# Moving the opening of a second transformer block into the last layer of the first

## The reference

```
x = layer_norm(DN_ALPHA * x + mix, ln1_g[l], ln1_b[l])
x = layer_norm(DN_ALPHA * x + swiglu(x, ffn_w1[l], ffn_w3[l], ffn_w2[l]), ln2_g[l], ln2_b[l])
```

```
mod   = silu(c)     @ w_ada + b_ada          # six parts of 1024: shift, scale, gate, twice
mod_c = silu(c_ctx) @ w_ada + b_ada
h_ctx = norm(ctx) * (1 + sc1c) + sh1c        # norm: plain layer norm, no gain, no bias
h_x   = norm(x)   * (1 + sc1)  + sh1
proj  = concat(h_ctx, h_x) @ w_in            # 512 tokens, 3936 columns
```

## Time and profile before

| what | value |
|---|---|
| time, median of 3 runs | 2152.38 us (2146.57, 2152.41, 2152.38) |
| time of the profiled execution | 2147.28 us |
| its span (first to last instruction) | 2145.2 us, so 2.08 us lie around it |
| PE, DVE, ACT, POOL busy | 95%, 40%, 22%, 12% of the span |
| mean granted TensorE clock | 0.979 of full speed |

### The profile page before, as it was taken

One profiled execution on the slowest core, in us unless ns is written; L12 is line 12 of the kernel. 1 busy time (PEld: TensorE's weight loads), 2 busy tenths in 40 slices (PEclk: granted clock), 3 DMA queues, 4 the chain that ended last, 5 costly groups with the idle time before them and its releaser, 6 DMA issues.

```text
span 2145.2 us, 33503 instructions
## 1 busy us (share of the span) xinstructions
PE 2046.7 (95%) x13831; PEld 1383.0 (64%) x13831; DVE 852.9 (40%) x1551; ACT 469.5 (22%) x881; POOL 250.7 (12%) x233
## 2 busy tenths in 40 slices
PE   8999999999999999999899999999997999999996
PEld 5678868864768868884445555899975444344342
DVE  1794220002379131000458847545557223323324
ACT  2254100000426201000132134432332110110110
POOL 2783000000478100000000002000000000000000
PEclk9999999999999999999899999999996999999998
DMA  7332544344533344435712333300013899999993
GB/s 240 118 118 99 201 152 151 124 168 133 175 118 118 116 179 157 157 118 180 262 70 79 118 118 124 114 4 4 3 44 136 353 410 395 393 395 411 394 392 143
DMA packets 138697, 385.37 MB, mean 180 GB/s; under 512 B 16935, under 2 KB 64399, under 8 KB 127441
## 3 DMA queue, kind: packets, MB, share of 16 engines
q1 hardware_dynamic: 138577, 383.61, 48.1%
HBM read 382.54 MB, written 1.05 MB: 179 GB/s over the span
## 4 chain that ended last, share of the span: by engine, by line
PE 42%; DVE 5%; ACT 2%; issue 1%; DMA 0%; DVEq 0%; POOL 0%; ACTq 0%; POOLq 0%
PE psum L1297 9%; PE psum L2874 9%; PE psum L2044 8%; PE psum L2898 5%; PE psum L2809 3%; PE psum L1496 1%; PE psum L2460 1%; ACT arena L1654 1%; PE psum L2113 1%; DVE arena L3087 1%; DVE arena L3009 1%; PE psum L2886 1%; PE psum L2062 1%; PE psum L2827 0%; DMA ring<-in_w_ada_dram 0%
## 5 line engine op out<-in xcount | busy, mean ns | idle before, releaser
L383 PE MATMUL psum<-arena,ring 128*128 128x256 f32 x1728 | 382.3, 380 | 1.0 <-ACT arena L666 1.0
L383 PEld LDWEIGHTS psum<-arena,ring 128*128 128x128 f32 x1728 | 324.5, 189 | 55.4 <-issue 8.6
L602 PE MATMUL psum<-arena,ring 128*128 128x256 f32 (+1 forms) x1536 | 306.8, 361 | 3.6 <-ACT arena L657 3.6
L602 PEld LDWEIGHTS psum<-arena,ring 128*128 128x128 f32 x1536 | 270.8, 190 | 39.3 <-issue 2.3
L2044 PE MATMUL psum<-arena 64*64 64x64 f32 (+1 forms) x4320 | 180.0, 237 | 4.2 <-DVE arena L2269 1.5
L2044 PEld LDWEIGHTS psum<-arena 64*64 64x64 f32 x4320 | 171.7, 134 | 6.3 <-issue 2.7
L666 ACT ACTIVATE arena<-psum 128x512 f32<-128x512 f32 (+2 forms) x100 | 54.4, 563 | 507.3 <-PE psum L602 264.1
L629 PE MATMUL psum<-ring,arena 128*128 128x512 f32 x352 | 151.7, 593 | 0.0
L1297 PE MATMUL psum<-arena,ring 128*128 128x512 f32 (+2 forms) x432 | 142.2, 489 | 0.0
L1067 DVE TENSOR_TENSOR arena<-arena,psum 128x512 f32<-128x512 f32 x22 | 15.2, 690 | 289.2 <-PE psum L602 289.2
L1297 PEld LDWEIGHTS psum<-arena,ring 128*128 128x128 f32 (+1 forms) x432 | 80.7, 187 | 61.3 <-issue 55.7
(11 more groups left out here) (418 smaller groups left out, 2585.5 us busy)
## 6 DMA issues: line engine op xcount, KB each, us to landing
ring<-in_w_in_dram SPq DMA_DIRECT2D x29, 2048.0 KB, 8.3
ring<-in_ffn_w_dram SPq DMA_DIRECT2D x46, 1024.0 KB, 5.5
arena<-in_ex_gate_dram SPq DMA_DIRECT2D x15, 2048.0 KB, 11.6
arena<-in_ex_up_dram SPq DMA_DIRECT2D x15, 2048.0 KB, 16.1
arena<-in_ex_down_dram SPq DMA_DIRECT2D x15, 2048.0 KB, 18.0
ring<-in_ex_gate_dram SPq DMA_DIRECT2D x14, 2048.0 KB, 10.9
ring<-in_ex_up_dram SPq DMA_DIRECT2D x14, 2048.0 KB, 15.4
ring<-in_ex_down_dram SPq DMA_DIRECT2D x14, 2048.0 KB, 8.1
```

The source lines that it names most:

```text
L383: ins = pe.matmul(bank[:, j, :], w[:, kc, c * P:(c + 1) * P], moving[:, kc, :], start=kc == 0, stop=kc == k - 1)
L602: ins = pe.matmul(bank[:, j, tokens], both[:, i * DC + kc, j * P:(j + 1) * P], K.xT[:, kc, tokens], start=kc == 0, stop=kc == DC - 1)
```

## The change

It moves parts of the second block's opening into the last layer and its feed-forward part:
- PE does the three transposes of the small rows after unit 3 of `ffn_w2`, into the two `next` banks; the eight `next` transposes no longer run in the last layer.
- ACT makes the conditioning vector right after the last `f1` drain (`mid_open_scalar`), and takes the root for the context norm.
- DVE does the whole context norm (`second_norm(0)`) before the last layer's second norm, and the second block's norm of token tile 0 (`second_norm(1)`) between that layer's norms of tile 0 and tile 1. Only tile 1 (`second_norm(2)`) is left for after it.
- ada units 0 and 1 are loaded into tiles that are dead by then (`K.early`), with no wait for a ring slot; the ring begins with ada 2, ada 3 and `w2in` 7, which are issued before the wait for the finished `x_in`.
- The transposes of `x` go by token tile; the gate columns are copied between the context's and `x`'s drains; POOL clears all but one tile earlier. Some tiles lie elsewhere, and the mid groups get other banks.

```diff
--- before.py
+++ after.py
@@ -635,14 +635,24 @@
         for u in range(W2_UNITS - 2):
             pe.wait_ge(K.landed(("w2", u)), K.landed_count(("w2", u), l))
             down(u, list(banks)).then_inc(K.used_up(("w2", u)), 1)
+        if l == DEPTH - 1:
+            pe.wait_ge(K.sem["dma_vec"], K.count("dma_vec"))
+            for i in range(2):
+                pe.wait_ge(K.empty(("next", i)), K.empty_count(("next", i), l))
+            pe.transpose(K.bank(("next", 0))[:, 0:P], K.vrows2, ident).then_inc(K.full(("next", 0)), 1)
+            bank = K.bank(("next", 1))
+            pe.transpose(bank[:, 0:P], K.crows[:, 0, :], ident)
+            n = 9 * CONV_CHUNKS - P
+            pe.transpose(bank[:, P:P + n], K.crows[0:n, 1, :], ident[0:n, 0:n]).then_inc(K.full(("next", 1)), 1)
         for u in range(W2_UNITS - 2, W2_UNITS):
             pe.wait_ge(K.landed(("w2", u)), K.landed_count(("w2", u), l))
             down(u, [(0, hf) for hf in range(2)])
...
-            pe.wait_ge(K.empty(("next", i)), K.empty_count(("next", i), l))
-            turn(("next", i), 0, i)
+        if l < DEPTH - 1:
+            for i in range(2):
+                pe.wait_ge(K.sem["x_in"], K.count("x_in", l, 2 * TT + i + 1))
+                pe.wait_ge(K.empty(("next", i)), K.empty_count(("next", i), l))
+                turn(("next", i), 0, i)
         for hf in range(2):
             down(W2_UNITS - 1, [(1, hf)])
         for i in range(2):
@@ -760,12 +770,16 @@
             if c >= 2:
                 act.wait_ge(K.empty(("f3", c - 2)), K.drained_count(("f3", c - 2), l))
...
+        if l == DEPTH - 1:
+            mid_open_scalar(act, K, l)
         for tt in range(TT):
             act.wait_ge(K.sem["x2_var"], K.count("x2_var", l, tt + 1))
             act.activation(K.x_std[:, tt:tt + 1], K.x_mv[:, tt, 1:2], ACT.Sqrt).then_inc(K.sem["x2_std"], 1)
-            if tt == 0:
+            if tt == 0 and l < DEPTH - 1:
                 for i in range(2):
                     turned_half(("next", i), l, 0, i)
+            if tt == 0 and l == DEPTH - 1:
+                second_std(act, K, 1)
 
 
 def layer_gpsimd(pool, K):
+                stats(x, K.nrm_mv[:, s, tt, :], K.bn2, 2)
+            var = K.nrm_mv[:, 0, :, 1] if n == 0 else K.nrm_mv[:, 1, n - 1:n, 1]
+            ts_op(var, var, LN_EPS_2, None, ALU.add).then_inc(K.sem["nrm_var"], 1)
+            dve.wait_ge(K.sem["nrm_std"], K.count("nrm_std", 0, n + 1))
+            std = K.nrm_std[:, 0, :] if n == 0 else K.nrm_std[:, 1, n - 1:n]
+            dve.reciprocal(std, std).then_inc(link.sem, 1)
+            dve.wait_ge(link.sem, link.count())
+            for x, s, tt in parts:
+                ins = ts_op(K.nrm[:, 1 - s, tt, :], x, K.nrm_mv[:, s, tt, 0:1], K.nrm_std[:, s, tt:tt + 1], ALU.subtract, ALU.mult)
+            ins.then_inc(K.sem["nrm"], 1)
+
         def norm(name, key, row, done):
             for tt in range(TT):
                 x = K.x_tok[:, tt, :]
         norm("x1", "mo", 0, "x1")
         for c in range(FFN_UNITS):
             dve.wait_ge(K.empty(("f1", c)), K.drained_count(("f1", c), l))
             dve.wait_ge(K.full(("f3", c)), K.full_count(("f3", c), l))
             tt_op(K.hT[:, 2 * c:2 * c + 2, :], pairs(K.silu[:, c % 2, :]), pairs(K.bank(("f3", c))), ALU.mult).then_inc(K.empty(("f3", c)), 1)
+        if l == DEPTH - 1:
+            dve.wait_ge(K.empty(("f3", FFN_UNITS - 1)), K.drained_count(("f3", FFN_UNITS - 1), l))
+            dve.wait_ge(K.sem["dma_ctx"], K.count("dma_ctx"))
+            second_norm(0)
         norm("x2", "f2", 2, "x_in")
-        link.end(DEPTH)
+        assert l == DEPTH - 1 or link.n == link.per
+    K.dve_base = (DEPTH - 1) * link.per + link.n
 
 
 
@@ -1093,17 +1130,18 @@
+EARLY = 2
 LATE = [4, 5, 10, 11, 6, 7, 8, 9]
...
+    return [("ada", c) for c in range(EARLY, 4)] + [("w2in", c) for c in (7, 3, 4, 2, 1, 0, 5, 6)] + [("ada", c) for c in LATE]
 
 
 def mid_groups():
-    keys = [("bvec", 0)]
@@ -1122,7 +1160,7 @@
 
 
 def mid_closes():
-    closes = {("mod_row", i): ("ada", i) for i in range(4)} | {("late_row", i): ("ada", c) for i, c in enumerate(LATE)}
...
@@ -1264,10 +1302,16 @@
 
     sp.wait_ge(K.sem["x1"], K.count("x1", DEPTH - 1))
     sp.dma_start(K.nrm[:, 1], A["ctx_2"][0].rearrange("(a p) d -> p a d", p=P)).then_inc(K.sem["dma_ctx"], 16)
-    for c in (0, 1, 2):
-        sp.wait_ge(K.used_up(("ada", c)), K.free_count(("ada", c)))
+    for c, landed in enumerate(("dma_ada_0", "dma_ada_1")):
         weights = rows(A["w_ada_2"])[:, :, c * BANK:(c + 1) * BANK]
-        sp.dma_start(K.slot_like(("ada", c), weights), weights).then_inc(K.landed(("ada", c)), 16)
+        sp.dma_start(K.early[:, c], weights).then_inc(K.sem[landed], 16)
+    for kind, c in mid_units()[0:3]:
+        sp.wait_ge(K.used_up((kind, c)), K.free_count((kind, c)))
+        if kind == "ada":
+            weights = rows(A["w_ada_2"])[:, :, c * BANK:(c + 1) * BANK]
+        else:
+            weights = rows(A["w_in_2"])[:, :, c * BANK:min((c + 1) * BANK, IN_2)]
+        sp.dma_start(K.slot_like((kind, c), weights), weights).then_inc(K.landed((kind, c)), 16)
     sp.wait_ge(K.sem["x_in"], K.count("x_in", DEPTH))
     sp.dma_start(K.wB, A["r_wB_2"][0].rearrange("z r n -> (z r) n")).then_inc(K.sem["dma_lora"], 16)
     sp.dma_start(K.aB[0:64, :], A["r_aB_2"][0]).then_inc(K.sem["dma_lora"], 16)
@@ -1318,14 +1367,6 @@
             at = 2 * (4 * i + q)
             ins = pe.matmul(bank[:, at:at + 2], rows[:, q * P:(q + 1) * P], K.sel, start=True, stop=True)
         return ins
-
-    pe.wait_ge(K.sem["dma_vec"], K.count("dma_vec"))
-    pe.wait_ge(K.empty(("bvec", 0)), K.empty_count(("bvec", 0)))
-    bank = K.bank(("bvec", 0))
-    pe.transpose(bank[:, 0:P], K.vrows2, ident)
-    pe.transpose(bank[:, P:2 * P], K.crows[:, 0, :], ident)
-    n = 9 * CONV_CHUNKS - P
-    pe.transpose(bank[:, 2 * P:2 * P + n], K.crows[0:n, 1, :], ident[0:n, 0:n]).then_inc(K.full(("bvec", 0)), 1)
 
     pe.wait_ge(K.sem["silu_c"], K.count("silu_c", 0, 1))
     pe.wait_ge(K.empty(("mod", 0)), K.empty_count(("mod", 0)))
@@ -1336,16 +1377,25 @@
             pe.wait_ge(K.empty(("mod_row", i - 1)), K.drained_count(("mod_row", i - 1)))
             ins = columns(K.bank(("mod", 0)), i - 1, K.hsT[:, i - 1, :])
     ins.then_inc(K.full(("mod", 0)), 1)
-    for s in range(2):
-        pe.wait_ge(K.sem["nrm"], K.count("nrm", 0, s + 1))
+    def turned(s, q, tt):
+        bank = K.bank(("hT", s, q)).rearrange("p (k n) -> p k n", k=2)
+        for j in range(2):
+            ins = pe.transpose(bank[:, j, tt * P:(tt + 1) * P], K.nrm[:, 1 - s, tt, (2 * q + j) * P:(2 * q + j + 1) * P], ident)
+        return ins
+
+    pe.wait_ge(K.sem["nrm"], K.count("nrm", 0, 1))
+    for q in range(4):
+        pe.wait_ge(K.empty(("hT", 0, q)), K.empty_count(("hT", 0, q)))
+        turned(0, q, 0)
+        turned(0, q, 1).then_inc(K.full(("hT", 0, q)), 1)
+    for tt in range(TT):
+        pe.wait_ge(K.sem["nrm"], K.count("nrm", 0, 2 + tt))
         for q in range(4):
-            pe.wait_ge(K.empty(("hT", s, q)), K.empty_count(("hT", s, q)))
-            bank = K.bank(("hT", s, q)).rearrange("p (k n) -> p k n", k=2)
-            for j in range(2):
-                for tt in range(TT):
-                    ins = pe.transpose(bank[:, j, tt * P:(tt + 1) * P],
-                                       K.nrm[:, 1 - s, tt, (2 * q + j) * P:(2 * q + j + 1) * P], ident)
-            ins.then_inc(K.full(("hT", s, q)), 1)
+            if tt == 0:
+                pe.wait_ge(K.empty(("hT", 1, q)), K.empty_count(("hT", 1, q)))
+            ins = turned(1, q, tt)
+            if tt == 1:
+                ins.then_inc(K.full(("hT", 1, q)), 1)
     for s in range(2):
         for q in range(4):
             pe.wait_ge(K.empty(("hT", s, q)), K.drained_count(("hT", s, q)))
@@ -1531,6 +1581,31 @@
                 yield dy, dx
 
 
+def second_std(act, K, n):
+
+    act.wait_ge(K.sem["nrm_var"], K.count("nrm_var", 0, n + 1))
+    std, var = ((K.nrm_std[:, 0, :], K.nrm_mv[:, 0, :, 1]) if n == 0 else
+                (K.nrm_std[:, 1, n - 1:n], K.nrm_mv[:, 1, n - 1:n, 1]))
+    act.activation(std, var, ACT.Sqrt).then_inc(K.sem["nrm_std"], 1)
+
+
+def mid_open_scalar(act, K, l):
+
+    for i, (dst, n) in enumerate(((K.vec2, P), (K.taps.rearrange("p t c -> p (t c)"), 9 * CONV_CHUNKS))):
+        act.wait_ge(K.full(("next", i)), K.full_count(("next", i), l))
+        act.activation(dst, K.bank(("next", i))[:, 0:n], ACT.Copy).then_inc(K.empty(("next", i)), 1)
+    for i in range(2):
+        act.wait_ge(K.empty(("next", i)), K.drained_count(("next", i), l))
+    col = lambda name, i=0, n=1: K.vec2[:, VROWS[name][0] + i:VROWS[name][0] + i + n]
+    act.activation(K.c_col[:, :, 0], col("c", 0, DC), ACT.Silu)
+    act.activation(K.c_col[:, :, 1], col("c_ctx", 0, DC), ACT.Silu).then_inc(K.link_act.sem, 1)
+    act.wait_ge(K.link_act.sem, K.link_act.count())
```

(68 more changed lines are left out.)

42 lines of the change are left out of this document (3 added, 39 removed).

## The result

The changed kernel took 2132.52 us (median of 4 runs, 2128.84 to 2134.89), the kernel before 2152.39 (median of 4, 2146.57 to 2155.93). The ratio is 0.9914, 95% interval 0.9892 to 0.9937: faster by 0.9%, between 0.6 and 1.1%. (The ratio is not the quotient of the two medians, which is 0.9908.) The prediction was 2134 us, range 2127 to 2144. The profiled execution has a span of 2132.9 us, against 2145.2.

A forecast was written before the change was run, and what follows sets the result against it. PE was taken to set the time; removing its idle and slow stretches before `lif` saves 16.0 us, giving 2131.3 from the profiled run or 2136.4 from the median; middle 2134 us, range 2127 to 2144.

The forecast's parts named there:

- The sum: From the last layer's end to `lif`: `lif` begins at 1062.4 instead of 1078.43, a saving of 16.0 us.
- Strips and columns: PE after the last layer's products: four units without pause at full clock, 11.36 us, ending at 1056.5.
- Transposes, drains, gate copies: Between columns and `lif`: transposes 1.04 us, DVE drains 3.86, gate copies 0.51, then 0.24 and some 0.3 of handing over.
- DVE's covers: Norms on DVE cost nothing: tile 0 takes 3.1 us, `mod` bank free 1 us early, tile 1 slack 5 us.
- rival of a late DVE: Tile 0's norm takes more than 4 us, holding PE before the first strips; at most 2 to 3 us lost; chance 0.05.
- The clock did not fall: Against rivals that it falls during strips and columns: at once, 4.7 us saved, chance 0.05; half-way, 11 saved, chance 0.08.
- a sign against strips and columns: In 1074 to 1076 PE was fully busy at clock 0.55; being busy had not raised it for some 12 us.
- The table load: ACT's context norm: a load takes 1.28 us; a further 1.38 us drain would end the norm near 1031.4, sum unchanged.
- Small rows, loads, lead: No PE wait near 1024; ada 3 lands at 1049.6, wanted at 1052.6; lead given back behind `lif`, chance 0.04.
- The check by segments: Same saving by PE pieces before `lif`: idle 5.54, first strips 1.89, ada 3's wait 2.84 and others, together 16.03 us.
- two levels: Whole-kernel runs before: two of three at the 2152.38 median, one at 2146.57; the forecast took the middle, 2134.

The follow-up runs named there:

- second measurement: The changed kernel run again with no edit, against the kernel before: 2134.0 us, ratio 0.9924.
- tight kernel: Changed kernel with `lif` waiting for drained banks pair by pair, `x` transposes bank by bank, gate copies ahead of modulation: 2130.63 us, ratio 0.9910 to before.

## Why the prediction was right, point by point

- **The sum.** Predicted 16.0 us: 0.55 ahead of the last product's end, and `lif` 17.3 us behind it. Measured: 16.76 us behind it, so with the 0.55 (worked out from rows, not measured by itself) the gain of the mechanism is 16.6. The medians' difference of 19.9 us is larger than that, but the ratio's interval, 0.63 to 1.08% of 2152 us or 14 to 23 us, holds 16.6; the second measurement gave a ratio 0.76% below 1, or 16.3 us, and medians 14.9 us apart.
- **Strips and columns**, 11.36 us predicted: 1048.07 to 1059.28, 11.2. ACT's drains never made PE wait.
- **Transposes, drains, gate copies**, 5.9 us predicted: 1059.28 to 1064.83, 5.5. The copies count on DVE's path between the drains and behind them alike (0.2 us apart). In the tight kernel, where they stand ahead of the modulation, they were done 0.9 us before it could begin.
- **DVE's covers.** Tile 0's norm took 3.2 us (1043.33 to 1046.58), predicted 3.1. The bank that `mod` needs was free 0.9 us before PE asked, predicted 1. The norm of tile 1 was ready 8.8 us after the last product, predicted 8.6. The rival of a late DVE did not come.
- **The clock did not fall.** PE entered the stretch busy and kept 1.00 throughout. The Trainium skill (TensorE: Matmul & The Clock Gate, What's actually happening) says that the default state is throttled and that activity releases the throttle; in this stretch the trace agrees. Taken plainly that sentence doesn't cover two other rows: 0.55 in 1074 to 1076 before, with PE busy since 1063.44, and 0.66 with PE busy for all 15 us in the last section. There the measurement decides. Pauses of 5.32, 4.00 and 2.98 us were followed by work at the lower level; so was the one of 2.77 us before, while one of 2.86 us was not, so the length alone does not decide. Nor does it say how long the low level lasts: behind 5.32 us it cost 1.8 us, behind the 2.77 us before, strips, columns and transposes took 6.0 us more than in the changed kernel. The work of that slow stretch ran at full clock once the pause ahead of it was gone, so what I had read as a sign against strips and columns was none at full clock; why the low level held there for so long stays open.
- **The table load.** In the changed kernel ACT loads the table for the root at 1028.49, off the path:

```profile
1028.49 1.28 ACT L1589 ACT_TABLE_LOAD   x1
1029.79 0.20 ACT L1589 ACTIVATE arena<-arena 128x2 f32<-128x2 f32 x1
```

  The load starts 0.01 us behind ACT's instruction before it, which ended at 1028.48, and the root 0.02 us behind the load. The further drain of about 1.38 us that the Trainium skill adds (ScalarE: Activation LUTs, What ACT_TABLE_LOAD costs) does not show here; the measurement decides.
- **Small rows, loads, lead.** No wait at 1026.7; ada 3, issued at 1044.7, landed 8.3 us later, 2.5 us before its strips (predicted 3.0), and no bracket names `w2in` 7; the 192.61 us piece is the same, so nothing was given back in it. From `lif` to the end the two profiles of the changed kernel took 1.3 and 0.9 us more than before; over all ten profiles this part took 1062.4 to 1069.3 us, and I did not trace why.
- **What was mis-sized.** The check by segments put 2.84 us down to the wait for ada 3 and most of the rest to vector and clock. It adds up, but it says where the time shows, not what carries it: without the early loads 13.5 of the 16.0 us are gone, without the early vector 7.1, without the early norms 5.4. These make 26 us, since each part opens the way for the others; vector alone brings 2.8 us, loads alone 8.3. Norms alone were not run. The DMA share of 98% in the window before hinted at the loads, and I had read it as background.
- **The level of the time, and luck.** I took the three times shown for two levels 5.8 us apart and set the forecast between 2131.3 and 2136.4. In 25 runs the kernel before lay anywhere from 2140.9 to 2155.7 us; there is no pair of levels. That 2134 lies within 1.5 us of the measured median is therefore luck: the gain of the medians was 3.9 us larger than the 16.0 forecast in this measurement, and 1.1 smaller in the next. What the traces bear out is the 16.0. The last section shows a source of the spread.

## What to carry to other kernels

Where several chains meet at the start of a stage, move all of them or price them jointly: here the vector alone bought 2.8 us of 16 and the loads alone 8.3, and the change without any one of the three lost 5 to 14. In a stretch whose DMA share is near one, count bytes: two units of 2 MB moved out of it were worth about their bytes over the measured rate, and a landing time of 8 us was 3 us too short where another unit was still landing. Then look for the windows ahead in which the DMA engines stand idle for want of a free tile; the moved loads fit there. A pause of PE of some 3 us was followed here by anything from no slow work to 6 us of it, so filling a pause can pay twice.
